# Block 1's recurrence: its gate matmuls in four groups of two tiles, their activations one panel later

## The chip, the cores and the metric

One Trainium2 chip, one of its cores. The engines are TensorE (PE), VectorE (DVE), ScalarE (ACT), GpSimd (POOL) and SyncE (SP). The metric is the device time of one execution in microseconds, the median of several runs.

## What is computed

Two transformer blocks in float32 over one sequence of 256 tokens, width 1024. The first has a compressed/windowed attention and, beside it, a gated linear recurrence; both come out of one input projection and are merged. The second has a gated feed-forward, two attentions and another feed-forward. The change touches the recurrence of the first block and, by the order of the queues, the attention beside it:

```python
def rg_lru_branch(xr, gate, conv_w, conv_b, w_a, b_a, w_i, b_i, lam):
    # xr (1, 256, 1024): causal conv of width 4, then 16 diagonal blocks of 64
    xc = conv(xr)
    r  = sigmoid(xc @ blockdiag(w_a) + b_a)
    ig = sigmoid(xc @ blockdiag(w_i) + b_i)
    log_a = -8 * r * softplus(-lam)
    a  = exp(log_a)
    bt = sqrt(-expm1(2 * log_a)) * (ig * xc)
    h  = scan(h[t] = a[t] * h[t-1] + bt[t])
    return h * gelu(gate)
```

## The kernel before, in words

Features lie on partitions in eight tiles of 128 (KT = 8, index t), tokens along the free axis (T = 256). All weights stream through the core as 158 **panels** of 128 x 2048 elements (1 MB). For a panel n, SP loads it into one of three raw buffers once the low half of panel n - 3 is made (`load`, L437 to L441); ACT copies it, rounded, to `wh` (`hi`, L1326 to L1334); DVE subtracts that from the raw panel and so makes the low half `wl` (`lo`, L1803 to L1806); PE waits for the low half (`split`, L688) and multiplies in three passes, high x high, low x high and high x low (L693 to L695), 48 matmuls of 256 columns or 24 of 512 to a panel.

PE, ACT and DVE each run a loop over the panel number n, written out by hand, in which everything else of the block has its place between the panels. The queues are in order. In round n, ACT makes the high copy of panel n + 2, which waits until panel n - 1 is done, and DVE the low half of panel n + 2. Panels 13 to 16 are the recurrence's gate branch, 17 to 20 and 21 to 24 the two merge gates, 25 and 26 the up-projection of the attention, 27 to 30 that of the recurrence. `CONV` is 12 and `CHAIN` 13, `GRP` 13, `GA` 17, `GB` 21, `UPA` 25, `UPR` 27.

The recurrence before:
- DVE, round 12 + t: `conv(t)` (L1945 to L1949), four ops.
- PE, behind panel 13 + t: the gate matmuls of tile t (L1058 to L1070), block-diagonal weights `bd`, plain float32, two matmuls that the trace shows as four records at L1068, into PSUM bank 2 + t % 2. They wait for `conv(t)` and for the ACT gates of tile t - 2, which read the same bank.
- ACT, round 14 + t: `lru_gates(t)` (L1426 to L1440), four ops: two Tanh of the two products (L1432, L1436), Exp (L1437), Tanh into `nth` (L1440). The last waits until DVE has used `nth` of tile t - 1 (`lru_q`). For t = 0 it stands behind the high copy, for the others at the round's end.
- DVE, round 14 + t, at its end: q of tile t (L2097 to L2102), two ops, the second of which frees `nth`.
- ACT, rounds 18 and 22 (`GA + 1`, `GB + 1`), L1538 to L1542: square roots of tiles 0 to 3 and 4 to 7. DVE, rounds 19 and 23: `recur` (L1955 to L1967), the scans and the product with the gate branch, four tiles at a time.
- ACT, round 25: the high part of the result (L1552); DVE, round 25, behind the low half of panel 27: its low part (L2115). PE waits for both of those before panel 27 (L1088).

The attention that lies beside it: PE turns the compressed probabilities behind panel 18 (L1041 to L1047, matmuls at L1045), which wait for DVE's round 18 (L2083 to L2088), and those for ACT's Exp in round 18 (L1517); ACT copies them at the head of round 19 (L1472); PE multiplies them behind panels 19 and 20 (L1055); DVE adds that to the attention's output behind the low halves of rounds 20 and 21 (L2092); PE turns the sum behind panel 22 (L1076), which waits for both additions; ACT and DVE split it in round 23 (`midh` L1545, `midl` L2105), for panel 25. L1513 and L1521 evacuate panels 11 to 16, L1531 is the Tanh of the merge gates. ACT switches its function table (ACT_TABLE_LOAD) where Gelu, Exp or Sqrt follow one another.

Of the kernel before, what the change touches and what calls it, by code (L numbers as in the profile page):

```python
# [21 lines left out]
T = 256  # L22
TT = T // P
D = 1024
KT = D // P
# [18 lines left out]
Q, KCVC, KSKW, VSVW, HEADS, GRP, GA, GB = 0, 2, 3, 4, 5, 13, 17, 21  # L44
XRS, CMPS = (5, 7, 9, 11), (6, 8, 10, 12)
CONV, CHAIN = 12, 13
UPA, UPR, WO, ML = 25, 27, 31, 35
ML_STEPS = 16
F1 = ML + 2 * ML_STEPS
# [51 lines left out]
def build(nc, a, out):  # L101
    ctx = ExitStack()
    with ctx:
# [57 lines left out]
        xc = carve(2080, KT, T)  # L161
# [525 lines left out]
        def _(pe):  # L687
# [275 lines left out]
            for n in range(KCVC, UPA):  # L963
# [84 lines left out]
                if n in (CHAIN + 6, CHAIN + 7):  # L1048
# [6 lines left out]
                        m = nc.tensor.matmul(ps[7 - tt][:, g * T:(g + 1) * T], pcT[:, tt * 2 + g, :],  # L1055
                                             vblk[:, g, :, :].rearrange("p r d -> p (r d)"), start=True, stop=True)
                    m.then_inc(oc_done, 1)
                if CONV + 1 <= n < CONV + 1 + KT:  # L1058

                    t = n - CONV - 1  # L1060
                    pe.wait_ge(conv_done, t + 1)
                    if t == 0:
                        pe.wait_ge(bd_loaded, 64)
                        pe.wait_ge(masked, NH)
                    if t >= 2:
                        pe.wait_ge(lru_act, t - 1)
                    for s in range(2):
                        m = nc.tensor.matmul(ps[2 + t % 2][:, s * T:(s + 1) * T], bd[:, t, s, :], xc[:, t, :],  # L1068
                                             start=True, stop=True)
                    m.then_inc(lru_done, 1)  # L1070
                if n == GB + 1:
                    pe.wait_ge(normed, NH)
                    pe.wait_ge(oc_read, 2)
# [244 lines left out]
        def _(act):  # L1318
# [7 lines left out]
            def hi(n):  # L1326


                act.wait_ge(panel_loaded[n % R], 16 * (n // R + 1))
                if n in (KSKW, VSVW):  # L1330
                    act.wait_ge(piece_loaded[n - KSKW], 16)
                if n >= R:
                    act.wait_ge(panel_done, n - R + 1)
                nc.scalar.activation(wh[:, n % R, :], raw[:, n % R, :], ACT.Copy).then_inc(hi_ready, 1)  # L1334
# [91 lines left out]
            def lru_gates(t):  # L1426

                if t == 0:
                    act.wait_ge(lru_consts, 1)
                act.wait_ge(lru_done, t + 1)  # L1430
                b = ps[2 + t % 2]
                nc.scalar.activation(igx[:, t, :], b[:, T:2 * T], ACT.Tanh, scale=0.5, bias=lru[:, 9, t:t + 1])  # L1432
                if t:

                    act.wait_ge(lru_act, t)
                link(nc.scalar.activation(thr[:, :], b[:, 0:T], ACT.Tanh, scale=0.5, bias=lru[:, 8, t:t + 1]))  # L1436
                nc.scalar.activation(abuf[:, t, :], thr[:, :], ACT.Exp, scale=lru[:, 6, t:t + 1], bias=lru[:, 6, t:t + 1])  # L1437
                if t:
                    act.wait_ge(lru_q, t)
                nc.scalar.activation(nth[:, :], thr[:, :], ACT.Tanh, scale=lru[:, 7, t:t + 1],  # L1440
                                     bias=lru[:, 7, t:t + 1]).then_inc(lru_act, 1)
# [15 lines left out]
            for n in range(ML):  # L1457
# [12 lines left out]
                if n == CHAIN + 6:  # L1470
                    act.wait_ge(pc_turned, 1)
                    nc.scalar.activation(pcT[:, :, :].rearrange("p a q -> p (a q)"), ps[7][:, :], ACT.Copy).then_inc(pcT_ready, 1)  # L1472
                hi(n + 2)
                if n == CONV + 2:
                    lru_gates(0)
                k = n - HEADS - 1
                if 0 <= k < NH:
# [55 lines left out]
                if n == GRP + 5:  # L1533
                    act.wait_ge(gr_evac, 4)
                    nc.scalar.activation(gru[:, :, :], gru[:, :, :], ACT.Gelu_apprx_tanh).then_inc(gr_gelu, 1)
                if 0 < n - CONV - 2 < KT:
                    lru_gates(n - CONV - 2)
                if n in (GA + 1, GB + 1):  # L1538
                    hf = (n - GA - 1) // 4
                    act.wait_ge(lru_q, 4 * hf + 4)  # L1540
                    q2 = xrp[:, 4 * hf:4 * hf + 4, 0:T]
                    nc.scalar.activation(q2, q2, ACT.Sqrt).then_inc(root_ready, 1)  # L1542
# [252 lines left out]
        def _(dve):  # L1795
# [159 lines left out]
            def recur(hf):  # L1955

                t0 = 4 * hf
                ts = slice(t0, t0 + 4)
                dve.wait_ge(root_ready, hf + 1)
                dve.wait_ge(gr_gelu, 1)  # L1960
                link(nc.vector.scalar_tensor_tensor(igx[:, ts, :], igx[:, ts, :], 1.0, xc[:, ts, :], ALU.add, ALU.mult))
                link(nc.vector.tensor_tensor(igx[:, ts, :], xrp[:, ts, 0:T], igx[:, ts, :], ALU.mult))
                for t in range(t0, t0 + 4):
                    m = nc.vector.tensor_tensor_scan(xc[:, t, :], abuf[:, t, :], igx[:, t, :], 0.0, ALU.mult, ALU.add)
                link(m)
                nc.vector.scalar_tensor_tensor(gru[:, ts, :], xc[:, ts, :], 0.5, gru[:, ts, :], ALU.mult,
                                               ALU.mult).then_inc(rnn_ready, 1)  # L1967
# [22 lines left out]
            for n in range(ML):  # L1990
# [103 lines left out]
                t = n - CONV  # L2094
                if 0 <= t < KT:
                    conv(t)
                t = n - CONV - 2  # L2097
                if 0 <= t < KT:
                    dve.wait_ge(lru_act, t + 1)
                    q2 = xrp[:, t, 0:T]  # L2100
# [2 lines left out]
                if n == GB + 2:  # L2103
# [2 lines left out]
                                            pair67[:, :, :].rearrange("p b c -> p (b c)"),  # L2106
                                            midh[:, 0:4, :].rearrange("p k t -> p (k t)").bitcast(F32),
                                            ALU.subtract).then_inc(midl_ready, 1)
                if n in (GA + 2, GB + 2):
                    recur((n - GA - 2) // 4)  # L2110
                if n == UPA:
                    for hf in range(2):
                        ts = slice(4 * hf, 4 * hf + 4)
# [385 lines left out]
```

## Time and profile before

| what | value |
|---|---|
| median of 3 runs (lowest to highest) | 954.9 us (954.88 to 955.16) |
| profiled execution, first to last instruction | 952.8 us, 13994 instructions |
| median less that span | 2.1 us |
| PE busy | 945.6 us |
| DVE, ACT, POOL busy | 666.5, 536.4, 63.1 us |
| DMA | 173.15 MB, mean 182 GB/s |
| mean granted TensorE clock | 0.998 of full speed |

The profiled execution's own time is known as its span alone; what lies around the span is taken from the median of the runs. Matmuls are pipelined, so that the times of two PE records overlap; their starts tell how fast PE goes. The pieces of the chain are drawn by ends and stand some 0.17 us later than the starts of the timeline.

### The profile page before, as it was taken

The page shows a single profiled execution, that of the slowest core. Times are in us where ns is not written, and L with a number is a line of the kernel's source. Part 1 is how long each engine was busy: PE and PEld are TensorE (multiplying, and loading weights), DVE is VectorE, ACT ScalarE, POOL GpSimd, SP SyncE. Part 2 cuts the span into 40 slices and gives each one's busy share as a digit, 9 for nine tenths or more (in the row PEclk, how much of TensorE's full clock was granted, in tenths as well). Part 3 has the DMA queues.
Part 4 walks back from the last instruction along what each step waited for, and adds up shares of the span by engine and source line. Part 5 has one row for each costly group of instructions (what it writes and reads, how often), then busy time and mean ns, then how long its engine had stood idle before and what let it go on. Part 6 is the DMA issues. An engine that isn't in the chain of part 4 may idle for free.

```text
span 952.8 us, 13994 instructions
## 1 busy us (share of the span) xinstructions
PE 945.6 (99%) x5420; PEld 829.0 (87%) x5420; DVE 666.5 (70%) x858; ACT 536.4 (56%) x691; POOL 63.1 (7%) x96
## 2 busy tenths in 40 slices
PE   9999999999999999999999999999999999999997
PEld 8999988888888888888888888999888898888886
DVE  6878869866665566588656666878887586565665
ACT  7677678435544444475445445679674464444544
POOL 1300000001000000022222000100100020000000
PEclk9999999999999999999999999999999999999999
DMA  9774344554765565547666655545445555655541
GB/s 299 238 237 135 131 133 152 204 178 129 254 206 182 196 198 176 178 160 237 210 214 197 216 177 177 167 145 176 133 133 177 177 183 193 215 182 182 191 156 44
DMA packets 119519, 173.15 MB, mean 182 GB/s; under 512 B 3184, under 2 KB 91520, under 8 KB 119472
## 3 DMA queue, kind: packets, MB, share of 16 engines
q1 hardware_dynamic: 117904, 168.32, 54.7%
q0 software_dynamic: 1424, 3.91, 1.4%
q8 instruction: 33, 0.54, 0.2%
q10 hardware_dynamic: 144, 0.26, 0.1%
q14 instruction: 14, 0.11, 0.0%
HBM read 171.44 MB, written 1.05 MB: 181 GB/s over the span
## 4 chain that ended last, share of the span: by engine, by line
PE 99%; DVE 0%; ACT 0%; issue 0%
PE pair L711 22%; PE pair L714 11%; PE acc L693 10%; PE acc L695 10%; PE acc L694 10%; PE pair L693 8%; PE pair L694 8%; PE pair L695 8%; PE acc L1068 1%; PE pair L921 1%; PE acc L1217 1%; PE pair L870 1%; PE acc L838 1%; PE acc L904 1%; PE acc L1242 1%; PE acc L1232 0%
## 5 line engine op out<-in xcount | busy, mean ns | idle before, releaser
L711 PE MATMUL pair<-actp,wh 128*128 128x512 f32 x912 | 292.7, 396 | 0.0
L1811 DVE TENSOR_TENSOR wl<-raw,wh 128x2048 fp32r<-128x2048 f32 x89 | 204.8, 2302 | 62.5 <-ACT wh L1340 62.5
L1340 ACT ACTIVATE wh<-raw 128x2048 fp32r<-128x2048 f32 x88 | 168.4, 1913 | 83.5 <-PE acc L695 83.5
L714 PEld LDWEIGHTS pair<-actp,wl 128*128 128x128 f32 x912 | 171.3, 188 | 39.9
L714 PE MATMUL pair<-actp,wl 128*128 128x256 f32 x912 | 179.2, 278 | 0.0
L1806 DVE TENSOR_TENSOR wl<-raw,wh 128x2048 fp32r<-128x2048 f32 x68 | 155.4, 2287 | 30.8 <-ACT wh L1334 30.3
L1334 ACT ACTIVATE wh<-raw 128x2048 fp32r<-128x2048 f32 x69 | 132.0, 1914 | 72.4 <-PE pair L695 47.8
L711 PEld LDWEIGHTS pair<-actp,wh 128*128 128x128 f32 x912 | 141.6, 189 | 1.4
L1559 ACT ACTIVATE arena<-pair 128x512 f32<-128x512 f32 x57 | 34.0, 597 | 170.8 <-PE pair L711 170.8
L693 PE MATMUL acc<-wh,midh 128*128 128x512 f32 x310 | 120.9, 390 | 0.0
L695 PE MATMUL acc<-wh,midl 128*128 128x512 f32 x310 | 120.6, 389 | 0.0
L694 PE MATMUL acc<-wl,midh 128*128 128x512 f32 x310 | 120.6, 389 | 0.0
L2161 DVE TENSOR_TENSOR arena<-pair,arena 128x512 f32<-128x512 f32 x57 | 39.4, 691 | 90.2 <-ACT arena L1559 90.2
L693 PE MATMUL pair<-actp,wh 128*128 128x256 f32 x248 | 71.5, 288 | 0.0
L695 PE MATMUL pair<-actp,wl 128*128 128x256 f32 x248 | 70.1, 283 | 0.0
L694 PE MATMUL pair<-actp,wh 128*128 128x256 f32 x248 | 70.1, 283 | 0.0
L694 PEld LDWEIGHTS acc<-wl,midh 128*128 128x128 f32 x310 | 58.2, 188 | 12.2
L695 PEld LDWEIGHTS acc<-wh,midl 128*128 128x128 f32 x310 | 58.2, 188 | 12.3
L693 PE MATMUL pair<-wh,actp 128*128 128x512 f32 (+1 forms) x176 | 68.2, 387 | 0.0
L693 PEld LDWEIGHTS acc<-wh,midh 128*128 128x128 f32 x310 | 58.2, 188 | 10.6
L695 PE MATMUL pair<-wh,actp 128*128 128x512 f32 (+1 forms) x176 | 66.9, 380 | 0.0
L694 PE MATMUL pair<-wl,actp 128*128 128x512 f32 (+1 forms) x176 | 66.9, 380 | 0.0
(371 smaller groups left out, 1395.2 us busy)
## 6 DMA issues: line engine op xcount, KB each, us to landing
raw<-in_w_in SPq DMA_DIRECT2D x35, 1024.0 KB, 5.2
raw<-in_mlp_w SPq DMA_DIRECT2D x32, 1024.0 KB, 5.2
raw<-in_ffn_w_gate SPq DMA_DIRECT2D x22, 1024.0 KB, 5.3
raw<-in_ffn_w_up SPq DMA_DIRECT2D x22, 1024.0 KB, 5.4
raw<-in_ffn_w_down SPq DMA_DIRECT2D x22, 1024.0 KB, 4.9
raw<-in_w_out SPq DMA_DIRECT2D x8, 1024.0 KB, 4.8
raw<-in_w_up_rnn SPq DMA_DIRECT2D x4, 1024.0 KB, 5.2
raw<-in_w_in SPq DMA_DIRECT2D x6, 512.0 KB, 6.2
```

The costliest lines, as they stand in the source:

```text
L693: nc.tensor.matmul(out_, lh, rh, start=start, stop=False, **kw)
L694: nc.tensor.matmul(out_, lh, rl, start=False, stop=False, **kw)
L695: return nc.tensor.matmul(out_, ll, rh, start=False, stop=stop, **kw)
L711: return nc.tensor.matmul(bank[:, :].rearrange("p (u t) -> p u t", u=2), h[:, k, cs], actp[:, :, k, :], **kw)
L714: return nc.tensor.matmul(bank[:, 0:T], l[:, k, cs], acth[:, k, :], **kw)
L838: m = nc.tensor.matmul(FIRST2[:, c, :], w[:, k, c * P:(c + 1) * P], x[:, k, :], start=k == 0 and w is h and x is acth, stop=stop and k == ...
L1334: nc.scalar.activation(wh[:, n % R, :], raw[:, n % R, :], ACT.Copy).then_inc(hi_ready, 1)
L1340: nc.scalar.activation(wh[:, n % R, :], raw[:, n % R, :], ACT.Copy).then_inc(hi_ready, 1)
L1559: return nc.scalar.activation(to, pair[:, :, T:2 * T], ACT.Copy)
L1806: nc.vector.tensor_tensor(wl[:, n % R, :], raw[:, n % R, :], wh[:, n % R, :].bitcast(F32), ALU.subtract).then_inc(lo_ready, 1)
L1811: nc.vector.tensor_tensor(wl[:, n % R, :], raw[:, n % R, :], wh[:, n % R, :].bitcast(F32), ALU.subtract).then_inc(lo_ready, 1)
L2161: return nc.vector.tensor_tensor(r, pair[:, :, 0:T], r, ALU.add)
```

## The change

The gate matmuls go from one tile behind each of panels 13 to 20 to two tiles behind each of panels 14, 16, 18 and 20. They wait for the convolution of both and for the ACT gates of all tiles before. ACT's gates of tile t go one round later: tile 0 to round 15 behind the high copy, tiles 1, 3, 5, 7 to the head of rounds 16, 18, 20, 22 ahead of the high copy, tiles 2, 4, 6 to the end of rounds 17, 19, 21. DVE's q goes to round 15 + t, the roots to rounds 19 and 23, the recurrences to rounds 20 and 24.

```diff
--- before.py
+++ after.py
@@ -44,6 +44,7 @@
 Q, KCVC, KSKW, VSVW, HEADS, GRP, GA, GB = 0, 2, 3, 4, 5, 13, 17, 21
 XRS, CMPS = (5, 7, 9, 11), (6, 8, 10, 12)
 CONV, CHAIN = 12, 13
+LRU_PANELS = range(CONV + 2, CONV + 10, 2)
 UPA, UPR, WO, ML = 25, 27, 31, 35
 ML_STEPS = 16
 F1 = ML + 2 * ML_STEPS
@@ -1055,19 +1056,20 @@
                         m = nc.tensor.matmul(ps[7 - tt][:, g * T:(g + 1) * T], pcT[:, tt * 2 + g, :],
                                              vblk[:, g, :, :].rearrange("p r d -> p (r d)"), start=True, stop=True)
                     m.then_inc(oc_done, 1)
-                if CONV + 1 <= n < CONV + 1 + KT:
-
-                    t = n - CONV - 1
-                    pe.wait_ge(conv_done, t + 1)
-                    if t == 0:
+                if n in LRU_PANELS:
+
+                    t0 = n - LRU_PANELS[0]
+                    pe.wait_ge(conv_done, t0 + 2)
+                    if t0 == 0:
                         pe.wait_ge(bd_loaded, 64)
                         pe.wait_ge(masked, NH)
-                    if t >= 2:
-                        pe.wait_ge(lru_act, t - 1)
-                    for s in range(2):
-                        m = nc.tensor.matmul(ps[2 + t % 2][:, s * T:(s + 1) * T], bd[:, t, s, :], xc[:, t, :],
-                                             start=True, stop=True)
-                    m.then_inc(lru_done, 1)
+                    else:
+                        pe.wait_ge(lru_act, t0)
+                    for t in (t0, t0 + 1):
+                        for s in range(2):
+                            m = nc.tensor.matmul(ps[2 + t % 2][:, s * T:(s + 1) * T], bd[:, t, s, :], xc[:, t, :],
+                                                 start=True, stop=True)
+                        m.then_inc(lru_done, 1)
                 if n == GB + 1:
                     pe.wait_ge(normed, NH)
                     pe.wait_ge(oc_read, 2)
@@ -1470,8 +1472,10 @@
                 if n == CHAIN + 6:
                     act.wait_ge(pc_turned, 1)
                     nc.scalar.activation(pcT[:, :, :].rearrange("p a q -> p (a q)"), ps[7][:, :], ACT.Copy).then_inc(pcT_ready, 1)
+                if n - 2 in LRU_PANELS:
+                    lru_gates(n - CONV - 3)
                 hi(n + 2)
-                if n == CONV + 2:
+                if n == CONV + 3:
                     lru_gates(0)
                 k = n - HEADS - 1
                 if 0 <= k < NH:
@@ -1533,10 +1537,10 @@
                 if n == GRP + 5:
                     act.wait_ge(gr_evac, 4)
                     nc.scalar.activation(gru[:, :, :], gru[:, :, :], ACT.Gelu_apprx_tanh).then_inc(gr_gelu, 1)
-                if 0 < n - CONV - 2 < KT:
-                    lru_gates(n - CONV - 2)
-                if n in (GA + 1, GB + 1):
-                    hf = (n - GA - 1) // 4
+                if n - 1 in LRU_PANELS[1:]:
+                    lru_gates(n - CONV - 3)
+                if n in (GA + 2, GB + 2):
+                    hf = (n - GA - 2) // 4
                     act.wait_ge(lru_q, 4 * hf + 4)
                     q2 = xrp[:, 4 * hf:4 * hf + 4, 0:T]
                     nc.scalar.activation(q2, q2, ACT.Sqrt).then_inc(root_ready, 1)
@@ -2094,7 +2098,7 @@
                 t = n - CONV
                 if 0 <= t < KT:
                     conv(t)
-                t = n - CONV - 2
+                t = n - CONV - 3
                 if 0 <= t < KT:
                     dve.wait_ge(lru_act, t + 1)
                     q2 = xrp[:, t, 0:T]
@@ -2106,8 +2110,8 @@
                                             pair67[:, :, :].rearrange("p b c -> p (b c)"),
                                             midh[:, 0:4, :].rearrange("p k t -> p (k t)").bitcast(F32),
                                             ALU.subtract).then_inc(midl_ready, 1)
-                if n in (GA + 2, GB + 2):
-                    recur((n - GA - 2) // 4)
+                if n in (GA + 3, GB + 3):
+                    recur((n - GA - 3) // 4)
                 if n == UPA:
                     for hf in range(2):
                         ts = slice(4 * hf, 4 * hf + 4)
```

## Rows read from the trace of the kernel before

**Rows 1.** The page: busy times by engine; the chain that ended last, by engine.
```profile
PE 945.6 (99%) x5420; PEld 829.0 (87%) x5420; DVE 666.5 (70%) x858; ACT 536.4 (56%) x691; POOL 63.1 (7%) x96
...
PE 99%; DVE 0%; ACT 0%; issue 0%
```

**Rows 2.** The chain in order of time: start, us, engine, tile, line.
```profile
96.87 1.06 PE acc L1068 x4
...
123.08 0.87 PE acc L1068 x4
...
143.40 0.86 PE acc L1068 x4
```

**Rows 3.** Timeline of PE: start, us, engine, line, operation, out<-in, shape, count.
```profile
122.80 0.28 PE L695 MATMUL pair<-actp,wl 128*128 128x256 f32 x1
...
123.59 0.58 PE L693 MATMUL acc<-wh,actp 128*128 128x512 f32 x1
...
124.02 0.39 PE L694 MATMUL acc<-wl,actp 128*128 128x512 f32 x1
...
135.62 0.60 PE L1045 MATMUL pair<-cst,xs 128*128 128x128 f32 x4
```

**Rows 4.** DMA issues of the page: KB each, median us to landing.
```profile
raw<-in_w_up_rnn SPq DMA_DIRECT2D x4, 1024.0 KB, 5.2
```

**Rows 5.** Timeline of ACT, rounds 17 and 18.
```profile
123.18 1.92 ACT L1334 ACTIVATE wh<-raw 128x2048 fp32r<-128x2048 f32 x1 [3.85 <-PE pair L695]
...
125.47 0.47 ACT L1432 ACTIVATE arena<-acc,lru 128x256 f32<-128x256 f32 x1
...
126.84 0.59 ACT L1440 ACTIVATE arena<-thr,lru 128x256 f32<-128x256 f32 x1
...
129.51 1.92 ACT L1334 ACTIVATE wh<-raw 128x2048 fp32r<-128x2048 f32 x1 [2.08 <-PE acc L695]
```

**Rows 6.** Timeline of DVE, rounds 17 and 18.
```profile
125.12 2.29 DVE L1806 TENSOR_TENSOR wl<-raw,wh 128x2048 fp32r<-128x2048 f32 x1 [3.05 <-ACT wh L1334]
...
130.43 0.43 DVE L2102 SCALAR_TENSOR_TENSOR arena<-arena 128x256 f32<-128x256 f32 x1
...
134.81 0.41 DVE L2088 TENSOR_TENSOR xs<-xs,small 128x240 f32<-128x240 f32 x1
```

**Rows 7.** Timeline of ACT, rounds 21 and 22.
```profile
157.80 0.60 ACT L1440 ACTIVATE arena<-thr,lru 128x256 f32<-128x256 f32 x1 [3.02 <-DVE arena L2102]
...
160.23 1.28 ACT L1542 ACT_TABLE_LOAD   x1
...
161.53 1.06 ACT L1542 ACTIVATE arena<-arena 128x1024 f32<-128x1024 f32 x1
```

**Rows 8.** Timeline of DVE, rounds 23 to 25.
```profile
168.89 1.22 DVE L1961 SCALAR_TENSOR_TENSOR arena<-arena 128x1024 f32<-128x1024 f32 x1
...
175.01 4.48 DVE L1806 TENSOR_TENSOR wl<-raw,wh 128x2048 fp32r<-128x2048 f32 x2
...
179.42 2.35 DVE L2115 TENSOR_TENSOR actp<-arena,actp 128x1024 fp32r<-128x1024 f32 x2
```

**Rows 9.** Timeline of PE, behind panel 22 and at panel 27.
```profile
162.18 1.03 PE L1076 MATMUL pair<-cst,arena 128*128 128x128 f32 x8
...
184.82 0.39 PE L693 MATMUL pair<-wh,actp 128*128 128x512 f32 x1
```

**Rows 10.** Timeline of ACT, then of PE, at the start of panel 13.
```profile
87.22 0.58 ACT L1513 ACTIVATE arena<-pair 128x512 f32<-128x512 f32 x1
...
88.14 0.28 PE L694 MATMUL pair<-actp,wh 128*128 128x256 f32 x1
```

**Rows 11.** Stretches: busy by engine (PE, PEld, DVE, ACT, POOL), clock, DMA, GB/s.
```profile
0.00:10.00 10.00, 8.75 (x35) 7.11 (x35) 4.52 (x11) 6.04 (x14) 4.09 (x9) 1.00 0.85 283
...
125.00:165.00 40.00, 40.00 (x185) 33.43 (x184) 32.83 (x45) 34.60 (x43) 0.00 (x0) 1.00 0.41 132
```

**Rows 12.** Group of the page: L870, idle before it in the last column.
```profile
L870 PE MATMUL pair<-arena 128*128 128x256 f32 x14 | 6.3, 644 | 1.2 <-DVE arena L1842 1.2
```

## The prediction

> **What bounds the kernel now.** I read, in this order: the busy shares and the chain that ended last [rows 1], the chain's pieces around the gate matmuls [rows 2], and the timelines of TensorE (PE), ScalarE (ACT) and VectorE (DVE) through panels 16 to 27 [rows 3]. PE is busy 99% of the span, and the chain is PE alone. So a change wins only by taking PE work or gaps away, and loses by making PE wait for something that is just in time now. This one takes no matmul away. What decides is the slack of ACT and DVE, which share the splitting of the panels (high copy L1334, low half L1806) with the recurrence.
>
> **PE's own part.** The group of four L1068 records between plain panels costs 0.87 us on the chain; behind L1055, work of its own kind, 0.86 [rows 2]: entering costs 0.01. Four of the eight groups lose their own entry and exit. The group after panel 13 costs 1.06 [rows 2], 0.19 more, behind the very short L1017 matmuls; panel 14 will stand behind those instead, and I expect it to pay the same. If the surplus belonged to the group, its 0.19 would go too. Bounds: 0 to 0.25 us gained; I take 0.05, nearest to the plain group.
>
> **What moves.** Panels 14, 16, 18 and 20 each start and end 0.87 us earlier, since the group ahead of them is gone; eight records follow each, so panels 15, 17, 19 and 21 start when they did. On ACT the gates of tiles 1, 3, 5 and 7 now stand at the head of rounds 16, 18, 20 and 22, ahead of the high copies of panels 18, 20, 22 and 24. A tile's gates end in an op (L1440) that waits for DVE's q of the tile before (`nth` has one buffer), and q now comes a round later, at the end of DVE's round. That is the added wait: every later high copy is queued behind it, and DVE's low halves and PE's panels behind those. SP only issues panel loads; each follows the low half of the panel three before and lands 5.2 us later [rows 4]. The closest is panel 27's: issued at 169.4 by the chain below, landed at 174.7, wanted at 175.9. I cost SP at nothing; if that 1.2 us were gone, the copy would slip by as much, ahead of a recurrence that keeps DVE busy anyway. POOL has nothing here.
>
> **First wait: L1045.** Panel 16's last matmul starts at 122.80, ACT's copy of panel 19 at 123.18 [rows 3, 5]. Both come 0.87 earlier: 122.31. DVE's round 17 starts at 124.25 instead of 125.12 and takes until the end of q, 130.43 + 0.43 - 125.12 = 5.74 us [rows 6]: q of tile 2 ends at 129.99. ACT needs 2.29 us for copy and evacuation (125.47 - 123.18), 1.86 for tile 2's gates and 1.37 for tile 3's first three ops (from L1432 to L1440, 126.84 - 125.47) [rows 5]; it is at tile 3's last op at 127.83 and waits until 130.02. With 0.49 for that op, the copy of panel 20 starts at 130.51, not 129.51 [rows 5]: 1.00 late. From that copy to the end of L2088, the compressed attention's probabilities, it is 134.81 + 0.41 - 129.51 = 5.71 us [rows 5, 6], so they are ready at 136.22. PE comes to L1045, which turns them, at 135.62 - 0.87 = 134.75 [rows 3], and waits 1.6 us with the latency. Before, it had 0.4 us of slack. Panel 19 starts 1.6 late.
>
> **The chain to panel 27.** I carried ACT's and DVE's queues forward in the order of the changed code, each instruction with its start-to-start time from these timelines, a table load with 1.30 to the next start [rows 7]. The same bookkeeping on the old order puts the second recurrence at 168.93 and the low halves of its result at 179.48; the rows have 168.89 and 179.42 [rows 8]. The new order gives:
> - ACT: copy of the turned probabilities 137.0, copy of panel 21 137.4, tile 4's gates 140.2, first root 144.8, tile 5's gates 147.2, copy of 22 at 149.0. As many table loads as before.
> - DVE: low half of 22 at 151.0 (panel 22 wants it at 158.3), the first attention sum 153.2, q 153.9, first recurrence 154.7 to 160.8 (6.12 us, 175.01 - 168.89 [rows 8]), low half of 23, the second sum until 163.75. L1076, at 162.18 now [rows 9] and 1.6 late, waits 0.1 to 0.2 for it, which doesn't add to the end.
> - ACT: tile 7's last op waits for q of tile 6 until 164.7, as it did until 157.80 [rows 7]; now the copy of panel 24 stands behind it (165.2), then copy 25 at 167.0, the other branch's gates 168.8, second root 171.2, `midh` 172.2, copy 26 at 173.2.
> - DVE: low half of 24 at 167.1, q 169.3, low half of 25 170.1, `midl` 173.2, low half of 26 175.1, second recurrence 177.3 to 183.45, low half of 27 until 185.65, the two L2115 until 187.96.
>
> Panel 27 needs the last of these. It starts at 184.82 now [rows 9]; already 1.6 late it would at 186.4. A release reaches PE's matmul after 0.22 us: L1513 ends at 87.80, and the panel's second matmul starts at 88.14, one pitch of 0.12 after the first [rows 10]. So it starts at 188.2, PE idles some 1.7 us, and is 3.3 to 3.4 us late in all. The low half of 28 is there at 191.4, before PE asks at 193.6; further on ACT and DVE idle in every round, so nothing more is lost, and nothing is won back, since PE has no slack. PE's 0.05 is inside the wait.
>
> **Sum.** Span 952.8 + 3.3 = 956.1. The runs' median of 954.9 is 2.1 above that span; with the same 2.1, **958.2 us**. From 122 to 188 us this is one string of ACT and DVE work: with every DVE time 2% shorter it gives +2.6, with every ACT time 2% shorter +2.7, both longer +4.3.
>
> **The rivals.** A measurement tells about 0.2% (1.9 us) from no change.
> - *Forecast, 0.72.*
> - *Only the first wait, 0.13.* L2115 ends at 181.77 and panel 27 starts at 184.82 [rows 8, 9]: 3.05 us of cover, and 1.6 more once PE is late. If the chain loses less than 4.6 us (I have 6.2), the second wait is nil: 956.5. For it speaks that DVE and ACT idle 3 us and more in several rounds, against it that they do so before the chain starts.
> - *No wait, 0.07.* If q of tile 2 were done by 127.8, the copy of panel 20 would keep its time and L1045 wait 0.7 at most: 954.8 to 955.6. Against it stand DVE's 5.74 us.
> - *Faster, 0.05.* Each return to panels may cost what the rows seem to show: the first matmul behind a group stands 0.43 ahead of its follower (123.59, 124.02 [rows 3]) where 0.23 is usual. Four returns at 0.2 and 0.19 of the first group make 1.0: 953.9, if ACT and DVE stay within L1045's 0.4 us of slack. The chain's 0.87 for a whole group speaks against it.
> - *A slower clock, 0.03.* The granted clock is 1.00, the 2.4 GHz level, here and in the first 10 us [rows 11], where L870 stood idle for 1.2 us [rows 12]. Should a wait of 1.6 bring it to 1.2 GHz for one panel, its 24 matmuls of 0.23 us take 5.4 us more: 963.6. The Trainium skill ("TensorE: Matmul & The Clock Gate", section "Why this matters for your kernels") says that long idle gaps between bursts bring the clock down; the rows have only a short gap, which didn't.
>
> A table load starts 1.30 us before the next instruction, 160.23 to 161.53 [rows 7]. The Trainium skill ("ScalarE: Activation LUTs", "What ACT_TABLE_LOAD costs") puts a drain of some 1.38 us on top of every switch. With the four switches on the chain that would make the forecast 5.5 us longer, an estimate; this trace disagrees.
>
> **The numbers.** The range holds the forecast's middle and reaches down to the first wait alone: 956.4 to 959.3. Outside are no wait, faster, the clock and the tails: 0.2. Faster by over 0.2%: 0.03, a part of its rival. Within 0.2%: 0.27, from no wait, only the first, the rest of faster and the forecast's lower tail. Slower: 0.70.
>
> **What would show it.** In the profile after, tile 3's last op idles 2.2 us for DVE and the copy of panel 20 starts near 130.5; L1045 starts near 136.4, with PE idle 1.6 ahead of it; tile 7's last op idles 7 to 8 us; the second recurrence starts near 177, and PE idles 1.7 ahead of panel 27. PE's busy time hardly moves. I am wrong if L1045 starts before 135.6, or if PE shows no gap before panel 27.

## The result, and the profile after

The changed kernel takes **958.02 us** (median of 5 runs, 957.73 to 959.71) where the kernel before takes 955.11 (5 runs on the same chip): ratio 1.0035, 95% interval 1.0025 to 1.0046, slower by 2.9 us. The profiled execution has a span of 955.8 us against 952.8 and took 957.91 itself, so 2.1 us again lie around the span.

The page after, busy times and the chain that ended last, for [rows 1]:

```profile
PE 946.0 (99%) x5420; PEld 828.7 (87%) x5420; DVE 666.4 (70%) x858; ACT 536.2 (56%) x691; POOL 63.0 (7%) x96
PE 92%; DVE 3%; ACT 3%; issue 1%; ACTq 0%
```

Every engine's busy time is within 0.4 us of before, yet the chain is no longer PE's alone: DVE and ACT now hold 6% of it. Where PE waited, in the stretch from 85 to 220 us (engine, tile, line, what it waited for: us in total, times, longest):

```profile
PE pair L1046 <- DVE xs L2092: 1.4, 1, 1.4
PE pair L694 <- DVE actp L2119: 1.2, 1, 1.2
```

The kernel before has neither. Line numbers have moved: L1045 is L1046 now, L1068 is L1070, L1076 is L1078, L693 to L695 are L694 to L696, ACT's L1334, L1432, L1437 and L1440 are L1336, L1434, L1439 and L1442, DVE's L1806, L2088, L2092, L2102 and L2115 are L1810, L2092, L2096, L2106 and L2119. This trace's times also run 0.23 us ahead of those of before: the second matmul of panel 13 is at 87.91, where [rows 10] has 88.14. I add 0.23 wherever I compare with a time of before or of the prediction.

The turned chain is the compressed attention's probabilities on their way through ACT and DVE to L1046, where PE turns them. ACT after, around it and around the copies of panels 22 and 24, for [rows 5, 7]:

```profile
122.08 1.91 ACT L1336 ACTIVATE wh<-raw 128x2048 fp32r<-128x2048 f32 x1 [5.14 <-PE pair L696]
...
127.09 0.60 ACT L1439 ACTIVATE xs<-thr,lru 128x256 f32<-128x256 f32 x1
129.79 0.60 ACT L1442 ACTIVATE arena<-thr,lru 128x256 f32<-128x256 f32 x1 [2.10 <-DVE arena L2106]
130.30 1.90 ACT L1336 ACTIVATE wh<-raw 128x2048 fp32r<-128x2048 f32 x1
...
145.65 1.28 ACT L1434 ACT_TABLE_LOAD   x1
...
148.32 0.59 ACT L1442 ACTIVATE arena<-thr,lru 128x256 f32<-128x256 f32 x1
148.81 3.70 ACT L1336 ACTIVATE wh<-raw 128x2048 fp32r<-128x2048 f32 x2
...
156.08 0.60 ACT L1439 ACTIVATE xs<-thr,lru 128x256 f32<-128x256 f32 x1
164.44 0.60 ACT L1442 ACTIVATE arena<-thr,lru 128x256 f32<-128x256 f32 x1 [7.75 <-DVE arena L2106]
164.95 3.70 ACT L1336 ACTIVATE wh<-raw 128x2048 fp32r<-128x2048 f32 x2
...
172.81 1.91 ACT L1336 ACTIVATE wh<-raw 128x2048 fp32r<-128x2048 f32 x1
```

Tile 3's last op (L1442) stands ready behind 127.09 and waits 2.10 us for DVE's q; the copy of panel 20 (130.30) is behind it. Tile 5's last op (148.32) waits for nothing, but its four ops and their table load stand ahead of the copy of panel 22, from 145.65 to 148.81; DVE idles 6.58 us for that copy, ahead of the first recurrence. Tile 7's last op waits 7.75 us for the q of tile 6, which DVE does behind that recurrence, and the copies of panels 24 and 25 (L1336 x2 at 164.95) are behind it.

DVE after, for [rows 6, 8]:

```profile
129.33 0.43 DVE L2106 SCALAR_TENSOR_TENSOR arena<-arena 128x256 f32<-128x256 f32 x1
132.23 2.29 DVE L1810 TENSOR_TENSOR wl<-raw,wh 128x2048 fp32r<-128x2048 f32 x1 [2.47 <-ACT wh L1336]
...
135.58 0.41 DVE L2092 TENSOR_TENSOR xs<-xs,small 128x240 f32<-128x240 f32 x1
...
150.74 2.29 DVE L1810 TENSOR_TENSOR wl<-raw,wh 128x2048 fp32r<-128x2048 f32 x1 [6.58 <-ACT wh L1336]
...
162.80 0.68 DVE L2096 TENSOR_TENSOR arena<-arena,pair 128x512 f32<-128x512 f32 x1
...
176.95 1.22 DVE L1965 SCALAR_TENSOR_TENSOR arena<-arena 128x1024 f32<-128x1024 f32 x1
...
181.94 1.23 DVE L1970 SCALAR_TENSOR_TENSOR arena<-arena 128x1024 f32<-128x1024 f32 x1
183.08 2.28 DVE L1810 TENSOR_TENSOR wl<-raw,wh 128x2048 fp32r<-128x2048 f32 x1
185.28 2.35 DVE L2119 TENSOR_TENSOR actp<-arena,actp 128x1024 fp32r<-128x1024 f32 x2
```

q of tile 2 is the row at 129.33, the probabilities of the turned chain that at 135.58, the second attention sum that at 162.80, the second recurrence begins at 176.95, and the low halves of its result (L2119) end at 187.63.

PE after, at the turned chain, at L1078 and at panel 27, for [rows 3, 9]:

```profile
134.25 0.39 PE L696 MATMUL acc<-wh,actp 128*128 128x512 f32 x1
136.04 0.66 PE L1046 MATMUL pair<-cst,xs 128*128 128x128 f32 x4 [1.41 <-DVE xs L2092]
136.54 1.89 PE L1070 MATMUL acc<-arena 128*128 128x256 f32 x8
138.08 0.58 PE L694 MATMUL pair<-wh,actp 128*128 128x512 f32 x1
138.50 0.40 PE L695 MATMUL pair<-wl,actp 128*128 128x512 f32 x1
...
163.38 0.39 PE L696 MATMUL acc<-wh,actp 128*128 128x512 f32 x1
163.63 1.06 PE L1078 MATMUL pair<-cst,arena 128*128 128x128 f32 x8
...
186.11 0.39 PE L696 MATMUL acc<-wh,midl 128*128 128x512 f32 x1
187.69 0.50 PE L694 MATMUL pair<-wh,actp 128*128 128x512 f32 x1 [1.19 <-DVE actp L2119]
188.03 0.39 PE L695 MATMUL pair<-wl,actp 128*128 128x512 f32 x1
```

At L1046 the start comes 1.79 us behind the last matmul, where it was 0.24 (135.38 to 135.62): 1.6 us late. At L1078 it comes 0.25 behind it (nothing), and the second matmul of panel 27 stands 1.92 behind the last of panel 26, not 0.45 (1.5 us late). That matmul is at 188.26 with the 0.23, and was at 185.05: 3.2 us later, which is the 3.0 of the span and the 0.23. The two waits make all but some 0.15 of it; that much gathers in steps of a few hundredths through panels 19 to 26, and no run tells why.

### The profile page after: what moved, and what is told of

It reads as the page before. It is cut to its first block, busy times and chain, and to the rows that moved or that the text cites. A ratio compares the mean times of both kernels' runs of the same rounds, so it can differ in the third digit from the quotient of the medians.

```text
span 955.8 us, 13991 instructions
## 1 busy us (share of the span) xinstructions
PE 946.0 (99%) x5420; PEld 828.7 (87%) x5420; DVE 666.4 (70%) x858; ACT 536.2 (56%) x691; POOL 63.0 (7%) x96
## 4 chain that ended last, share of the span: by engine, by line
PE 92%; DVE 3%; ACT 3%; issue 1%; ACTq 0%
PE pair L712 22%; PE pair L715 11%; PE acc L694 9%; PE acc L696 9%; PE acc L695 9%; PE pair L694 7%; PE pair L696 7%; PE pair L695 7%; ACT wh L1336 1%; DVE wl L1810 1%; PE pair L922 1%; PE acc L1219 1%; PE acc L839 1%; PE pair L871 1%; PE acc L905 1%
## 5 line engine op out<-in xcount | busy, mean ns | idle before, releaser
L1810 DVE TENSOR_TENSOR wl<-raw,wh 128x2048 fp32r<-128x2048 f32 x68 | 155.5, 2288 | 36.7 <-ACT wh L1336 36.3
L1336 ACT ACTIVATE wh<-raw 128x2048 fp32r<-128x2048 f32 x69 | 131.7, 1913 | 62.5 <-PE pair L696 42.9
L694 PE MATMUL acc<-wh,midh 128*128 128x512 f32 x310 | 120.9, 390 | 0.0
L696 PE MATMUL acc<-wh,midl 128*128 128x512 f32 x310 | 120.6, 389 | 0.0
L695 PE MATMUL acc<-wl,midh 128*128 128x512 f32 x310 | 120.6, 389 | 0.0
L694 PE MATMUL pair<-actp,wh 128*128 128x256 f32 x248 | 71.3, 288 | 0.0
L696 PE MATMUL pair<-actp,wl 128*128 128x256 f32 x248 | 70.1, 283 | 0.0
L695 PE MATMUL pair<-actp,wh 128*128 128x256 f32 x248 | 70.1, 283 | 0.0
L694 PE MATMUL pair<-wh,actp 128*128 128x512 f32 (+1 forms) x176 | 68.3, 388 | 1.2 <-DVE actp L2119 1.2
L695 PEld LDWEIGHTS acc<-wl,midh 128*128 128x128 f32 x310 | 58.2, 188 | 12.2
L696 PEld LDWEIGHTS acc<-wh,midl 128*128 128x128 f32 x310 | 58.2, 188 | 12.2
L694 PEld LDWEIGHTS acc<-wh,midh 128*128 128x128 f32 x310 | 58.2, 188 | 10.7
L696 PE MATMUL pair<-wh,actp 128*128 128x512 f32 (+1 forms) x176 | 66.9, 380 | 0.0
L695 PE MATMUL pair<-wl,actp 128*128 128x512 f32 (+1 forms) x176 | 66.9, 380 | 0.0
```

What stands on the lines that cost most here:

```text
L694: nc.tensor.matmul(out_, lh, rh, start=start, stop=False, **kw)
L695: nc.tensor.matmul(out_, lh, rl, start=False, stop=False, **kw)
L696: return nc.tensor.matmul(out_, ll, rh, start=False, stop=stop, **kw)
L1810: nc.vector.tensor_tensor(wl[:, n % R, :], raw[:, n % R, :], wh[:, n % R, :].bitcast(F32), ALU.subtract).then_inc(lo_ready, 1)
```

## The experiments

Each was timed against the kernel before on its own chip, in three groups on three chips: e1 to e4 (its median there 954.70), e5 to e8 (954.65), e9 to e12 (954.67). The changed kernel itself was not timed on these; its 2.9 us over before is from the result's chip. Waits are those of each kernel's one profiled execution. "Theory" in the expectations is the prediction's: ACT and DVE together are one string of work that sets PE's two waits. Diffs are against the changed kernel unless said otherwise.

### Is it the grouped matmuls, or the order on ACT and DVE?

**e1_act_dve_only**: ACT and DVE in the new order, PE with its gate matmuls one tile behind each panel, as before.

```diff
-                if n in LRU_PANELS:
-...
-                    for t in (t0, t0 + 1):
+                if CONV + 1 <= n < CONV + 1 + KT:
+                    t = n - CONV - 1
+                    pe.wait_ge(conv_done, t + 1)
...
```

> ACT and DVE as changed, PE's gate matmuls back to one tile behind each of panels 13 to 20. Theory (the string of ACT and DVE work behind the new wait sets the time, the grouping on PE only helps it start earlier): as slow as the change or slower, since panel 16 again ends 0.87 us later: +4.2 us over the kernel before, L1045's counterpart waits 1.7 us, the turning of the attention's sum 0.9 to 1.1, panel 27 1.2 to 1.5. Rival (the grouping of the matmuls on PE is what costs): back to the kernel before, within 0.5 us.

Measured 959.07 us, ratio 1.0047 (1.0033 to 1.0060): 4.4 over before. PE's waits:

```profile
PE pair L1046 <- DVE xs L2091: 1.4, 1, 1.4
PE pair L694 <- DVE actp L2118: 1.2, 1, 1.2
PE pair L1077 <- DVE arena L2095: 0.8, 1, 0.8
```

The two waits are there, as long as in the changed kernel, with no grouping at all. So the order on ACT and DVE is enough for the loss. In this order grouping on PE even gives something back, since the panels whose ends release ACT (14, 16, 18) then end 0.87 sooner: 0.8 us by the extra wait at L1077, 1.5 by the medians (4.4 less 2.9, on two chips); the difference of the two is not explained. Grouping on PE with the old order on ACT and DVE was not run.

**e4_group_first**: the group behind panel 18 goes ahead of the turned chain on PE, to fill the first wait.

```diff
-                if n == CHAIN + 5:
-                    pe.wait_ge(pc_ready, 1)
-...
                 if n in (CHAIN + 6, CHAIN + 7):
...
                         m.then_inc(lru_done, 1)
+                if n == CHAIN + 5:
+                    pe.wait_ge(pc_ready, 1)
+...
```

> The changed kernel with the order behind panel 18 turned round on PE: first the eight gate matmuls, then the turning of the compressed probabilities. Theory (one string, the gaps on PE are where it touches PE): PE no longer idles at L1046's counterpart, but the string is not shortened, so panel 20 to 22 come earlier only to make PE wait 1.9 us for the attention's sum behind panel 22, and 1.2 to 1.5 before panel 27: total as the change, +3.2 us. Rival (two independent waits that add): the first 1.6 us are won, total +1.4 us.

Measured 958.38 us, ratio 1.0039 (1.0025 to 1.0053): 3.7 over before.

```profile
PE pair L1078 <- DVE arena L2096: 1.6, 1, 1.6
PE pair L694 <- DVE actp L2119: 1.2, 1, 1.2
```

The first wait is filled, and it comes back at L1078 at 1.6 us: PE's order can't win what the string does not give. The expectation had 1.9 there and 3.2 over before; the rival had 1.4. The 0.5 us above the expectation is not explained.

### Which of ACT's waits?

**e2_two_nth**: a second buffer for the gates' last step, so that it waits for q of two tiles before.

```diff
         nth = carve(9760 + T, T)
+        nths = [nth, carve(9760, T)]
...
-                if t:
-                    act.wait_ge(lru_q, t)
+                if t > 1:
+                    act.wait_ge(lru_q, t - 1)
...
```

> The changed kernel with a second buffer for nth, so that the last gate op of tile t waits for q of tile t - 2 and in practice for nothing. Theory: that op no longer idles (2.1 and 7.8 us before), the copy of panel 20 starts when panel 17 is done, the wait at L1046 shrinks from 1.7 to 0.7 us, panel 27 does not wait: +0.9 us over the kernel before. Rival (the round by which the recurrence is later is what makes panel 27 wait): the gap before panel 27 stays at 1.2 us or more, total +2 us or more.

Measured 955.61 us, ratio 1.0009 (1.0000 to 1.0018): 0.9 over before, as expected. One wait of PE is left, 0.4 us where the expectation had 0.7:

```profile
PE pair L1047 <- DVE xs L2093: 0.4, 1, 0.4
```

**e3_tile5_behind_copy**: tile 5's gates behind the copy of panel 22 instead of ahead of it.

```diff
-                if n - 2 in LRU_PANELS:
+                if n - 2 in LRU_PANELS and n != CONV + 8:
                     lru_gates(n - CONV - 3)
                 hi(n + 2)
+                if n == CONV + 8:
+                    lru_gates(n - CONV - 3)
```

> The changed kernel with tile 5's gates behind the copy of panel 22 instead of ahead of it; nothing else. Theory: the wait at L1046 stays (1.7 us), the copy of 22 and with it the first recurrence come 3 us earlier, the gap before panel 27 and the short one before the turning of the attention's sum are gone: +1.7 us over the kernel before. Rival (panel 27's gap comes from tile 7's op and the copy of 24 behind it alone): gap before panel 27 unchanged, +3.2.

Measured 956.49 us, ratio 1.0017 (1.0008 to 1.0026): 1.8 over before. The wait at L1046 stays at 1.4 us and that of panel 27 is gone. The copy of panel 22 starts at 145.67 and the second recurrence at 174.52, less the 0.15 by which this trace runs behind the changed kernel's: 3.3 and 2.6 us earlier than there.

**e9_q_first**: only the order on DVE is altered, q ahead of the conv of the same round.

```diff
-                t = n - CONV
-                if 0 <= t < KT:
-                    conv(t)
                 t = n - CONV - 3
...
+                t = n - CONV
+                if 0 <= t < KT:
+                    conv(t)
```

> The changed kernel with DVE's q ahead of the conv of the same round, and nothing else. Theory (this removes the 2.1 us for which ACT holds tile 3's last step, and leaves the hold of tile 5's, which lies behind the low half of panel 22): the wait at the turned chain falls from 1.4 to 0.4 us, that of panel 27 stays at 1.2, and the time is 2.0 to 2.5 us over before. Rival (the order on DVE was the whole fault, and both waits go): 0.4 to 0.8 over before, as with both orders altered.

Measured 956.85 us, ratio 1.0021 (1.0012 to 1.0030): 2.2 over before, with a wait of 0.4 us at L1046 and of 1.2 at panel 27.

**e5_q_first_tile5**: the edits of e3 and e9 together.

> The changed kernel with two orders altered and no buffer more: DVE computes a tile's q ahead of the conv of the same round, and ACT issues tile 5's gates behind the copy of panel 22. Theory (the waits of the changed kernel come from two places in ACT's queue: tile 3's last step, held by DVE's q behind the conv, and tile 5's, held by the low half of panel 22): the wait at the turned chain (L1046) falls from 1.4 to 0.7 us, the wait of panel 27 goes whole, ACT's wait for the last q shrinks to about 4.9 us once, and the time is 0.7 us over the kernel before (0.3 to 1.1), so 2.5 us under the changed kernel. Rival (grouping itself costs on PE, in groups of eight with other work between them): at least 1.6 us over before, as with tile 5 moved alone.

Measured 955.31 us, ratio 1.0002 (0.9993 to 1.0011): 0.7 over before.

```profile
PE pair L1046 <- DVE xs L2094: 0.4, 1, 0.4
```

**e10_two_nth_q_first**: the edits of e2 and e9 together.

> The changed kernel with two buffers for the gates' last step by turns and q ahead of conv. Theory: with the second buffer ACT no longer waits for q at all, so the order on DVE has nothing left to give: within 0.2 us of the kernel with the second buffer alone, 0.7 to 1.1 over before, with the one wait of 0.4 us at the turned chain. Rival (the two act on different waits and add up): no wait left at the turned chain, 0.0 to 0.3 over before.

Measured 955.34 us, ratio 1.0005 (0.9997 to 1.0014), 0.7 over before, and again a wait of 0.4 us at L1046. The second buffer had already taken what q's order can give.

So each wait has its own place on ACT. The order on DVE takes 1 us from the first, tile 5's place takes the second away, and the second buffer does both. The expectations of e5 and e9 say that tile 5's last op is held; no trace shows that. The second wait needs two things together: tile 5's gates ahead of the copy of panel 22, and tile 7's last op held behind the recurrence that is late for it. In e2 the copy of panel 22 still starts late (148.31, in a trace 0.48 behind the changed kernel's), and as nothing holds tile 7's op the wait is gone all the same.

The 0.4 us that none of them removes is 0.6 from start to start (in e9 134.18 to 134.99, less 0.24), and 0.7 in the time: it is the 0.87 by which PE comes earlier to the turned chain, less its slack. In e9 the copy of panel 20 starts at 129.22 with 0.29 to add, which is the 129.51 of before, so what PE waits for there is not late; PE is early. That part does come from the grouping. None of these beats the kernel before, and with PE busy 99% of the span there was little to win.

### One string, or separate waits?

**e8_tile3_behind_copy**: tile 3's gates behind the copy of panel 20 and the exponential of the turned chain.

```diff
-                if n - 2 in LRU_PANELS:
+                if n - 2 in LRU_PANELS and n != CONV + 6:
                     lru_gates(n - CONV - 3)
...
+                if n == CONV + 6:
+                    lru_gates(n - CONV - 3)
                 if GRP < n <= GRP + 4:
```

> The changed kernel with tile 3's gates (the group behind panel 18) issued by ACT behind the copy of panel 20 and the exponential of the turned chain; everything else, tile 5 among it, as in the changed kernel. Theory (one string: what the copy of panel 20 gains, tile 3's gates lose, and the later rounds take it over): the wait at L1046 falls from 1.4 to 0.7 us, the wait at the carried recurrence (L1078) grows from 0.0 to about 1.0, that of panel 27 stays at 1.2 to 1.5, and the total is 0.2 us under the changed kernel (3.0 to 3.4 over before). Rival (each wait stands for itself): 0.7 to 1.0 us under the changed kernel.

Measured 957.51 us, ratio 1.0026 (1.0016 to 1.0036): 2.9 over before, as the changed kernel itself and just under the 3.0 to 3.4 expected. The rival would have been at 1.9 to 2.2.

```profile
PE pair L694 <- DVE actp L2121: 1.2, 1, 1.2
PE pair L1078 <- DVE arena L2098: 0.6, 1, 0.6
PE pair L1046 <- DVE xs L2094: 0.4, 1, 0.4
```

Of the 1.0 us that the first wait lost, 0.6 reappears at L1078, where the theory had all of it.

**e7_before_three_sums**: in the kernel before, the sum over the probabilities (L2083, 0.40 us on DVE, in the round of panel 18) is issued three times more for nothing, 1.31 us in all.

```diff
                     link(nc.vector.tensor_reduce(small[:, 24:40], pcv, AX_X, ALU.add))
+                    link(nc.vector.tensor_reduce(small[:, 24:40], pcv, AX_X, ALU.add))
...
```

> The same three idle sums (1.3 us of DVE work in the round of panel 18) in the kernel before. Theory (the kernel before has 0.2 to 0.5 us to spare at the turned chain, and over 6 us at panel 27): PE waits 0.8 to 1.1 us at L1045 and at no other place, and the time is 0.8 to 1.1 us over before. Rival (the round of panel 18 had more to spare, and the changed kernel's wait there comes from the grouped matmuls, not from work ahead of the chain): no wait, within 0.3 us of before.

Measured 955.49 us, ratio 1.0011 (1.0002 to 1.0020): 0.8 over before, with one wait, of 0.8 us at L1045. The kernel before had 1.31 less 0.8, some 0.5 us, to spare there (0.35 counted from start to start) and enough at panel 27.

**e6_after_three_sums**: the same three sums in the changed kernel.

> The changed kernel with the 0.40 us sum over pc (one DVE instruction of the turned chain, in the round of panel 18) issued four times, three of them for nothing: 1.3 us more DVE work ahead of the turned chain and of q. Theory (from there on one string of ACT and DVE work without slack sets PE's waits, so that what is late at the turned chain is late at panel 27 too, and once only): the wait at L1046 grows from 1.4 to 2.7 us, that at panel 27 stays at 1.2 to 1.6, and the time is 1.3 us over the changed kernel (4.2 to 4.8 over before). Rival (the two waits are independent of one another and the second has a fixed source of its own): the second wait shrinks by as much as the first grows, and the total does not change.

Measured 958.97 us, ratio 1.0040 (1.0026 to 1.0053): 4.3 over before, 1.4 more than the changed kernel's 2.9. The total is the theory's. The waits of the profiled execution are not: only one is left, and panel 27 no longer waits. PE in its timeline:

```profile
135.99 0.39 PE L696 MATMUL acc<-wh,actp 128*128 128x512 f32 x1
139.10 0.66 PE L1046 MATMUL pair<-cst,xs 128*128 128x128 f32 x4 [2.72 <-DVE xs L2095]
139.59 3.40 PE L1070 MATMUL acc<-arena 128*128 128x256 f32 x8
...
143.21 0.41 PE L695 MATMUL pair<-wl,actp 128*128 128x512 f32 x1
...
190.76 0.39 PE L696 MATMUL acc<-wh,midl 128*128 128x512 f32 x1
190.98 0.39 PE L694 MATMUL pair<-wh,actp 128*128 128x512 f32 x1
191.21 0.39 PE L695 MATMUL pair<-wl,actp 128*128 128x512 f32 x1
```

and the stretches around it, in the columns of [rows 11] (the granted clock is the third number from the end):

```profile
136.00:138.00 2.00, 0.38 (x2) 0.00 (x0) 1.86 (x6) 1.46 (x1) 0.00 (x0) 1.00 0.30 49
138.00:140.00 2.00, 0.90 (x6) 0.88 (x7) 1.82 (x7) 0.21 (x1) 0.00 (x0) 0.95 1.00 372
140.00:142.00 2.00, 2.00 (x7) 1.53 (x6) 1.66 (x4) 2.00 (x2) 0.00 (x0) 0.50 0.27 103
142.00:144.00 2.00, 2.00 (x8) 1.58 (x7) 1.78 (x1) 1.98 (x6) 0.00 (x0) 0.69 0.00 0
```

Behind the pause of 2.72 us the granted clock went to 0.50, the 1.2 GHz level, from 139.8 to 143.2. The eight gate matmuls span 3.40 us, not 1.89. From the start of L1046 to panel 19's second matmul it is 4.11 us, in the changed kernel 2.46: 1.65 us lost to the clock (the next expectation has 1.87, which these rows do not bear out). PE reaches panel 27 so late that its operand is already there. Against the changed kernel, with the 1.75 us by which this trace starts later taken off, panel 27's second matmul is 191.21 - 188.03 - 1.75 = 1.43 us late: the DVE string's 1.31 and a tenth that the clock put on top.

This holds for the profiled execution alone. It took 960.84 us, 1.9 over the median, and 1.75 of that lies ahead of panel 13, where nothing was altered. Of the other four, three have a mean granted clock of 0.999. A fall of 3.4 us to one half takes 1.7 us out of the 957, or 0.0018 off that mean, so those three can't have had it; they took 958.87, 958.87 and 958.97, the total that the theory gives without any fall. Where they waited no trace shows.

### Does the clock's fall cost anything where no later wait covers it?

**e11_tile5_three_sums** joins e3's edit with e6's, so that panel 27 gives no cover; **e12_tile5_two_sums** has two more sums in place of three.

> The changed kernel with tile 5's gates behind the copy of panel 22 (which left the wait at the turned chain, 1.41 us, alone) and with the sum over pc issued three more times (1.31 us of DVE work). In the changed kernel with the three sums the wait of 2.72 us was followed by 3 us at a granted clock of 0.50 to 0.95, the eight gate matmuls and the first of panel 19 took 1.87 us longer, and panel 27 no longer waited, so that the total showed only 1.4 of these 3.2 us. Theory (the clock falls behind the long wait and the 1.9 us are real, only covered there by the wait of panel 27, which then starts late anyway): here nothing covers them, so 1.31 + 1.87 = 3.2 us over the kernel with tile 5 moved alone, 5.0 over before (4.6 to 5.4). Rival (the low clock is of that one profiled execution or costs nothing in the total): 1.3 over it, 3.1 over before.

> The same with two more sums (0.87 us), so that PE waits 2.28 us at the turned chain, between the 1.41 us that left the granted clock at 1.00 and the 2.72 us behind which it fell. If the clock stays: 0.9 us over the kernel with tile 5 moved alone, 2.6 to 2.8 over before. If it falls as it did behind 2.72 us: 0.9 + 1.9 = 2.8 over it, 4.5 over before. No row tells which; the length lies nearer to the 2.72 us, so the fall is the likelier.

e11 took 958.53 us (957.18 to 960.42; ratio 1.0037, 1.0025 to 1.0049), e12 958.96 (957.20 to 959.86; 1.0039, 1.0026 to 1.0052): 3.9 and 4.3 over before, and the one with less work is not the faster. Stretches of e12:

```profile
134.00:136.00 2.00, 0.70 (x4) 0.24 (x2) 1.90 (x5) 1.78 (x1) 0.00 (x0) 1.00 0.16 27
136.00:138.00 2.00, 1.01 (x5) 1.02 (x6) 1.82 (x7) 0.00 (x0) 0.00 (x0) 0.70 0.97 334
138.00:140.00 2.00, 2.00 (x6) 1.56 (x6) 1.54 (x4) 1.86 (x2) 0.00 (x0) 0.50 0.42 164
140.00:142.00 2.00, 2.00 (x10) 1.68 (x9) 1.44 (x1) 2.00 (x5) 0.00 (x0) 0.95 0.00 0
```

The clock fell behind 2.29 us of waiting as it did behind 2.72, and stayed low for 3.4 us again. By the count above it cost 1.55 us in e12 and 1.51 in e11; in e11 the clock was not yet back at that matmul, and counted two matmuls further it is 1.66. In both profiled executions the whole of it reaches the end. The span of e11 is 957.1, that of e3 954.5, and e11's trace starts panel 13 0.31 earlier: 2.9 us longer, where 1.31 + 1.66 makes 3.0. For e12 it is 956.8 and 0.08: 2.4, where 0.87 + 1.55 makes 2.4.

The medians say less. Neither reaches the theory's full sum (for e11 1.8 + 1.3 + 1.65, so 4.75), nor does e11 stay at the rival's 3.1. The executions of e11 spread over 3.2 us and those of e12 over 2.7, those of e3 over 0.8. With the mean granted clock e11's run 1.000: 957.18; 0.998: 957.25, 958.15, 958.97; 0.997: 958.90; 0.995: 960.42. The one at 1.000 had no fall. The others can't be sorted so: the mean also holds the last few us, in which the clock is low in the kernel before too (0.50 from 950 us on, mean 0.998), e12's profiled execution with its fall has 0.998 as well, and another of e12 took 959.60 at 0.998. The lowest of e12, 957.20, fits e3's 956.49 and the 0.87 us of sums without a fall; the lowest of e11, 957.18, is 0.6 under e3 and its sums, which no row explains. So the clock does not fall in every execution. How often it does, and how much of the spread is its, six and five executions cannot tell.

## Why the prediction was right

The time came out at 958.0 for 958.2, slower as forecast at 0.70, by the two waits that were named. The totals stand closer than the differences, and that is luck: forecast was 3.3 us over a kernel before of 954.9, measured 2.9 over one of 955.1 (3.2 from panel 13 to panel 27 in the traces).

- **First wait.** Forecast: q of tile 2 ends at 129.99, copy of panel 20 at 130.51, probabilities at 136.22, a wait of 1.6. Measured, with the 0.23: 129.99, 130.53 and 136.22, and 1.6 from start to start (1.4 as the profile counts the wait). Confirmed also by e9 (q earlier takes 1 us of it) and e2 (no hold by q).
- **The chain to panel 27.** Forecast low half of 22 at 151.0, copy of 24 at 165.2, of 26 at 173.2, second recurrence at 177.3, end of the low halves at 187.96, PE at 188.2; measured 150.97, 165.18, 173.04, 177.18, 187.86 and 187.92. The order that the prediction wrote down held in every row; after 60 us it was off by 0.1 us on DVE and 0.3 at PE's start. Of this 0.3 the larger part is the term for a release, put at 0.22 from the end of an ACT record: behind DVE's L2119 the matmul's record starts 0.06 later (187.63 to 187.69), behind L2092 0.05 (135.99 to 136.04), and counted over the second matmul, as the prediction did, it is 0.17. e3 and e2 show the two links that the chain turned on, tile 5's gates ahead of the copy of panel 22 and the op of tile 7 that holds the copy of panel 24.
- **L1078.** Forecast a wait of 0.1 to 0.2 that doesn't add; the record shows none (0.25 from start to start). It was priced too high by that much, without effect.
- **PE's own part.** Forecast 0.05 gained, with the surplus of the first group passed on to panel 14. The surplus did pass on: from the start of the short matmuls (L1017, then L1018) to panel 14's second matmul it was 2.09 us with a group between and is 1.23 without, so the group took 0.86 and not 1.06. The gain did not come: panel 17's first matmul starts at 123.59 before and at 123.36 + 0.23 = 123.59 after.
- **The rivals.** "Only the first wait" is what e3 and its 956.5 look like: right in its price, wrong for this kernel, since the chain lost more than the cover. "No wait" fell with 1.6 us at L1046. "Faster" fell too: with all but 0.4 us of the waits gone (e5, e10) the grouped kernel is no faster than before, and panel 17, behind two of the four groups, starts when it did.
- **The clock.** The pauses of 1.4 and 1.2 us left the granted clock at 1.00 in the profiled execution of the change, so this rival did not happen. Its price was too high: 5.4 us for a whole panel, where the falls behind 2.3 to 2.7 us took in eight gate matmuls and little more and cost 1.5 to 1.7. The Trainium skill's sentence that the prediction cites ("TensorE: Matmul & The Clock Gate", "Why this matters for your kernels": long idle gaps between bursts bring the clock down) agrees with the profiled executions of e6, e11 and e12.
- **The table loads.** The copies behind the four switches came within 0.2 us of a count that gave each load 1.30 us. The drain of some 1.38 us that the Trainium skill states ("ScalarE: Activation LUTs", "What ACT_TABLE_LOAD costs") would have put them up to 5.5 us later, an estimate; this trace disagrees again: the load at 145.65 ends at 146.93 and the next op starts at 146.94.

## What to carry to other kernels

When work is moved on a saturated kernel, cost the order of the queues and not the work: an instruction that waits holds all that is behind it, and here two small ops that wait for another engine's result cost 2 of the 2.9 us with no busy time changed (e2 takes their waits away and is 0.9 over before). Carry both queues forward row by row until they idle again, and look for the next operand that PE needs just in time; a wait filled in one place can come back at the next (e4 whole, e8 in part). If two engines hand single buffers to one another, a second buffer or the order within a round is a cheap mend; here neither made the change pay.

## What the runs showed of the hardware that was not expected

In three profiled executions (e6, e11, e12) a pause of PE of 2.3 to 2.7 us in an otherwise dense stretch was followed by some 3.4 us at half the clock, at a price of 1.5 to 1.7 us; pauses of 1.2, 1.4 and 1.6 us (the changed kernel, e4) left the granted clock at 1.00. The price shows in the total only where no later wait covers it: e11 and e12 paid it whole, while e6 lost 1.65 us to the clock and still ended where the DVE string put it. The mean granted clock of an execution is a poor sign of such a fall, since the idle end of the program lowers it as much.

Executions of one kernel also differ for another reason than the clock. The profiled executions of e1, e6, e8 and e10 start panel 13 1.2 to 1.8 us later than that of the changed kernel does, at a granted clock of 1.00 up to there and though nothing ahead of it was altered, and each took 1.3 to 1.9 us more than its kernel's median. The eleven executions of e7, with a pause of 0.8 us only, spread over 2.4 us. So the wide spread of e11 and e12 is no proof of the clock by itself.
